# Five weight slots whose residual overwrites the raw weight, in place of four slots and a ring of two raw buffers

## The chip, the cores and the metric

The kernel runs on one core of a Trainium2 chip. The metric is the device time of one execution in microseconds, taken as the median of the runs shown. All arithmetic is float32; matmuls run on float32 operands rounded to the reduced format fp32r.

## What is computed

A batch of one sequence of 256 tokens with 2048 features passes three blocks. The first block has one layer, the second has two, each with an own set of weights. Cut to what matters:

```python
# first block
z = rms_norm(x) @ w_in                      # 2048 x (2048,2048,2048,512,512,2048,2048,2048)
u, g, q, k, v, g_attn, m_lru, m_attn = split(z)
u = depthwise_conv(u); h = rg_lru(u, forward) + rg_lru(u, backward)
y_a = h * silu(g)
y_b = windowed_gqa(rope(q), rope(k), v, sink) * silu(g_attn)
merged = sigmoid(m_lru) * (y_a @ w_proj_a) + sigmoid(m_attn) * (y_b @ w_proj_b)
x = x + rms_norm(merged @ w_out)
# second block, two layers
h = rms_norm_2(x) @ w_in
a = sliding_window_sink_attention(...); b = conformer_conv_module(...)   # 31 taps
c = gated_deltanet(...)                                                  # chunks of 64
x = x + concat(a, b, c gated by silu) @ w_out
```

Nearly all of the arithmetic is the products with the weights. To keep float32 accuracy each product is made of three matmuls: `x_hi*w_hi + x_lo*w_hi + x_hi*w_lo`, where `w_hi` is the weight rounded to fp32r and `w_lo = w - w_hi` is its residual, and the same for x.

## The kernel before

The weights lie in DRAM as 288 slots of 128 x 2048 floats (1 MB): 152 of the first block (`SLOTS_1`), then 68 for each layer of the second (`SLOTS_2`). The class `Ring` streams them. For each slot n there are four steps, each on an engine of its own and each in program order on it:

- `load` (SP): a DMA of slot n from DRAM into one of two raw buffers (`w_raw`, `RAW = 2`). It waits until the residual of slot n-2 is done (semaphore `split`), since that slot was the last to use the same raw buffer.
- `round` (ScalarE, line 273): copies `w_raw` into `w_hi[n % 4]`, rounded. It waits for the transfer (`loaded0`, `loaded1`) and until TensorE has finished slot n-4 (`used`), which had the same `w_hi` and `w_lo`.
- `residual` (VectorE, line 280; in four parts at line 291 in one stage): `w_lo[n % 4] = w_raw - w_hi`. It waits for the rounding.
- `features`, `tokens`, `halves` or `last_tokens` (TensorE, lines 309, 321, 345, 333): 48 matmuls of 256 columns or 24 of 512. They wait for `split` of slot n and increase `used` at the end.

The four steps are placed by hand in each engine's program, `round` and `residual` three slots ahead of the matmuls, between the operations of the stage. The stages of the first block are LRU (slots 0 to 31, in 8 passes of four with gate matmuls at line 1112 after each), keys and values (32 to 39), attention (40 to 71), two gating products and two projections (72 to 135) and the output projection (136 to 151). Those of each later layer, counted from its first slot: C (0 to 7, the input of the 31-tap convolution), KV (8 to 11), Q (12 to 17), ZA (18 to 23), D (24 to 41, the inputs of the delta rule, with the heads' softmax, flips at line 2602, the sum over the convolution at 2623 and the products at 2613 in between), ZB (42 to 45), ZC (46 to 51, with the delta rule's chains of small matmuls and transposes, line 2700 among them) and OUT2 (52 to 67). Between the blocks the first three slots of the next layer are loaded, rounded and split by the block before it.

SP's program holds all transfers in order, also those of constants, gate weights, the stream x that is stored and read back (`x_t`), and waits of its own: for `gates` ahead of each set of gate weights, for `joined` ahead of the store of x between the blocks, for `used` and `added` ahead of the loads and stores of `x_t`. All DMAs go through one queue.

Other names in the rows: L1089 turns the first x; L1112 multiplies by the gate weights and reads `u_all`, which L828 and L832 make (the short convolution); L2501 turns x at the start of the second block; L2540 multiplies the keys `q_raw` by the turning matrix and reads `q_sq`, which L1668 makes; L1755 copies the softmax weights `S` for L2613; L1793 makes `sq` for L2619; L1773 and L2202 make the delta rule's short convolution; L2045 makes the taps of the long one; L1884 scales the keys of the delta rule, and L2234 makes `yb_now`, for which line 2700 waits before its second use.

Of the kernel before, what the change touches and what calls it, by code (L numbers as in the profile page):

```python
# [9 lines left out]
F32 = mybir.dt.float32  # L10
# [14 lines left out]
SLOTS = 4  # L25
RAW = 2
# [220 lines left out]
class Ring:  # L247


    def __init__(self, k, s, first, ready=0, last=None, since=None):  # L250
        self.k, self.s, self.first, self.ready, self.last = k, s, first, ready, last
        self.since = since or record(loaded0=0, loaded1=0, rounded=0, split=0, used=0)
        self.loaded = (s.loaded0, s.loaded1)
        self.odd = 1 if since else 0

    def load(self, sp, n):
        n -= self.ready
        if n < 0 or n + self.ready >= self.last:
            return
        if self.since.split or n >= 2:  # L260
            sp.wait_ge(self.s.split, self.since.split + n - 1)
        raw = (n + self.odd) % RAW
        sp.dma_start(self.k.w_raw[:, raw], self.k.w[self.first + self.ready + n]).then_inc(self.loaded[raw], 16)

    def round(self, act, n):
        if n < self.ready or n >= self.last:
            return
        m = n - self.ready
        raw = (m + self.odd) % RAW
        act.wait_ge(self.loaded[raw], (self.since.loaded1 if raw else self.since.loaded0) + 16 * (m // 2 + 1))  # L270
        if self.since.used or n >= SLOTS:
            act.wait_ge(self.s.used, self.since.used + n - SLOTS + 1)
        act.activation(self.k.w_hi[:, n % SLOTS], self.k.w_raw[:, raw], ACT.Copy).then_inc(self.s.rounded, 1)  # L273

    def residual(self, dve, n):
        if n < self.ready or n >= self.last:
            return
        m = n - self.ready
        dve.wait_ge(self.s.rounded, self.since.rounded + m + 1)
        dve.tensor_tensor(self.k.w_lo[:, n % SLOTS], self.k.w_raw[:, (m + self.odd) % RAW], self.k.w_hi[:, n % SLOTS].bitcast(F32),  # L280
                          ALU.subtract).then_inc(self.s.split, 1)

    def residual_part(self, dve, n, part):
# [3 lines left out]
        m = n - self.ready  # L287
        here = slice(512 * part, 512 * part + 512)
        if part == 0:
            dve.wait_ge(self.s.rounded, self.since.rounded + m + 1)  # L290
        ins = dve.tensor_tensor(self.k.w_lo[:, n % SLOTS, here], self.k.w_raw[:, (m + self.odd) % RAW, here],
                                self.k.w_hi[:, n % SLOTS, here].bitcast(F32), ALU.subtract)
# [3 lines left out]
    def await_slot(self, pe, n):  # L296
        if self.since.split or n >= self.ready:
            pe.wait_ge(self.s.split, self.since.split + n - self.ready + 1)

    def features(self, pe, n, out, x_hi, x_lo, each=None, whole=True):  # L300

        w_hi, w_lo = (w[:, n % SLOTS].rearrange("p (k f) -> p k f", k=KT) for w in (self.k.w_hi, self.k.w_lo))
# [9 lines left out]
    def tokens(self, pe, n, quarter, outs, x_hi, x_lo):  # L312

        w_hi, w_lo = (w[:, n % SLOTS].rearrange("p (k f) -> p k f", k=4) for w in (self.k.w_hi, self.k.w_lo))
# [9 lines left out]
    def last_tokens(self, pe, n, outs, x_hi, x_lo, first_half):  # L324

        w_hi, w_lo = (w[:, n % SLOTS].rearrange("p (k f) -> p k f", k=4) for w in (self.k.w_hi, self.k.w_lo))
# [9 lines left out]
    def halves(self, pe, n, half, outs, x_hi, x_lo):  # L336

        w_hi, w_lo = (w[:, n % SLOTS].rearrange("p (k f) -> p k f", k=8) for w in (self.k.w_hi, self.k.w_lo))
# [28 lines left out]
B1_SEMS = ("loaded0 loaded1 rounded split used "  # L367
# [9 lines left out]
def first_parts(k, t, s):  # L377
# [4 lines left out]
    ring = Ring(k, s, 0, 0, SLOTS_1 + SLOTS - 1)  # L382
# [78 lines left out]
    def sync(sp):  # L461
# [10 lines left out]
        ring.load(sp, 2)  # L472
# [5 lines left out]
        for n in range(3, SLOTS_1 + SLOTS - 1):  # L478
            ring.load(sp, n)
# [809 lines left out]
    "loaded0 loaded1 rounded split used "  # L1289
    "p2_in turn_in soft_in narrow_in cumulate_in levels_in "  # L1290
# [1834 lines left out]
```

## Time and profile before

| | us |
|---|---|
| median of 3 runs | 1966.73 |
| lowest, highest | 1965.78, 1968.35 |
| the profiled execution's own time | 1965.31 |
| its span, first to last instruction | 1963.5 |
| granted TensorE clock, mean | 0.993 |
| TensorE matmul busy | 1917.0 |
| VectorE busy, ScalarE busy | 1263.2, 1105.6 |

The profiled execution took 1.8 us more than its span and 1.4 us less than the median. In the rows that follow, PE is TensorE, DVE is VectorE, ACT is ScalarE, SPq is the queue that issues the DMAs; times are microseconds from the start of the span.

### The profile page before, as it was taken

The numbers are of one execution on the slowest core, as the hardware profiler recorded it, in microseconds if no ns is written. First come the engines' busy times: TensorE is split into PE (matmuls) and PEld (weight loads), VectorE is DVE, ScalarE is ACT, GpSimd is POOL, SyncE is SP. The second block draws the span as 40 slices with busy tenths as digits, with TensorE's granted clock in tenths as the row PEclk, the third lists the DMA queues.
The fourth block names the chain that finished last, engine by engine and source line by source line (L and its number), as shares of the span: only waits on it lengthen the run. The fifth ranks groups of instructions, "written<-read, shape, count | busy, mean of one in ns | idle before, by whom it ended". The sixth has DMA issues, their size and how long they took to land.

```text
span 1963.5 us, 32526 instructions
## 1 busy us (share of the span) xinstructions
PE 1917.0 (98%) x13840; PEld 1726.0 (88%) x13840; DVE 1263.2 (64%) x1771; ACT 1105.6 (56%) x1506; POOL 69.8 (4%) x66
## 2 busy tenths in 40 slices
PE   7999999999999999999899999999999999999998
PEld 6999989999888888888899999898889999888887
DVE  5877856555444444654698988655558888865553
ACT  6777755555543333434656588825464657874451
POOL 0111100000000000000000101100000000010000
PEclk9999999999999999999999999999999999999999
DMA  6444454444455555565544443323555443342153
GB/s 234 181 186 174 160 215 172 154 150 149 177 188 200 193 194 194 184 257 193 204 162 158 161 146 134 120 76 112 213 198 215 164 170 131 131 148 87 66 206 137
DMA packets 52272, 328.61 MB, mean 167 GB/s; under 512 B 7968, under 2 KB 10144, under 8 KB 14368
## 3 DMA queue, kind: packets, MB, share of 16 engines
q1 hardware_dynamic: 52128, 326.54, 46.0%
q8 instruction: 109, 1.79, 0.4%
q14 instruction: 35, 0.29, 0.0%
HBM read 320.23 MB, written 6.29 MB: 166 GB/s over the span
## 4 chain that ended last, share of the span: by engine, by line
PE 83%; DVE 7%; ACT 5%; DMA 3%; issue 2%; SPq 0%; DVEq 0%; ACTq 0%
PE z L321 36%; PE z L309 33%; DMA w_raw<-in_w_dram 3%; DVE w_lo L280 2%; ACT w_hi L273 2%; PE aux L2734 1%; PE aux L1112 1%; DVE conv L2202 1%; PE z L333 1%; DVE acc L2045 1%; PE aux L2739 1%; PE aux L1160 1%; PE aux L2632 1%; PE aux L1177 1%; PE z L345 1%
## 5 line engine op out<-in xcount | busy, mean ns | idle before, releaser
L280 DVE TENSOR_TENSOR w_lo<-w_raw,w_hi 128x2048 fp32r<-128x2048 f32 x274 | 631.2, 2305 | 429.0 <-ACT w_hi L273 428.7
L273 ACT ACTIVATE w_hi<-w_raw 128x2048 fp32r<-128x2048 f32 x286 | 547.7, 1917 | 493.4 <-PE z L321 234.2
L309 PE MATMUL z<-xn_hi,w_hi 128*128 128x256 f32 x2112 | 621.3, 294 | 1.5 <-DVE w_lo L280 0.9
L309 PE MATMUL z<-xn_lo,w_hi 128*128 128x256 f32 x2112 | 598.7, 283 | 0.0
L309 PE MATMUL z<-xn_hi,w_lo 128*128 128x256 f32 x2112 | 598.6, 283 | 0.0
L309 PEld LDWEIGHTS z<-xn_hi,w_hi 128*128 128x128 f32 x2112 | 406.0, 192 | 18.5 <-issue 13.0
L309 PEld LDWEIGHTS z<-xn_lo,w_hi 128*128 128x128 f32 x2112 | 406.4, 192 | 5.0 <-issue 4.3
L309 PEld LDWEIGHTS z<-xn_hi,w_lo 128*128 128x128 f32 x2112 | 405.9, 192 | 0.0
L321 PE MATMUL z<-w_hi,xn_hi 128*128 128x512 f32 x568 | 222.9, 393 | 0.0
L321 PE MATMUL z<-w_hi,xn_lo 128*128 128x512 f32 x568 | 221.1, 389 | 0.0
L321 PE MATMUL z<-w_lo,xn_hi 128*128 128x512 f32 x568 | 221.1, 389 | 0.0
L321 PE MATMUL z<-w_hi,y_hi 128*128 128x512 f32 x368 | 143.6, 390 | 0.0
L321 PE MATMUL z<-w_hi,y_lo 128*128 128x512 f32 x368 | 143.3, 389 | 0.0
L321 PE MATMUL z<-w_lo,y_hi 128*128 128x512 f32 x368 | 143.2, 389 | 0.0
L321 PEld LDWEIGHTS z<-w_hi,xn_lo 128*128 128x128 f32 x568 | 106.6, 188 | 22.3
L321 PEld LDWEIGHTS z<-w_lo,xn_hi 128*128 128x128 f32 x568 | 106.7, 188 | 21.6
L321 PEld LDWEIGHTS z<-w_hi,xn_hi 128*128 128x128 f32 x568 | 106.7, 188 | 21.7
L2045 DVE SCALAR_TENSOR_TENSOR acc<-padded_b,params,acc 128x256 f32<-128x256 f32 x240 | 98.8, 476 | 0.0
L321 PEld LDWEIGHTS z<-w_hi,y_lo 128*128 128x128 f32 x368 | 69.1, 188 | 14.4
L321 PEld LDWEIGHTS z<-w_lo,y_hi 128*128 128x128 f32 x368 | 69.1, 188 | 14.1
L321 PEld LDWEIGHTS z<-w_hi,y_hi 128*128 128x128 f32 x368 | 69.1, 188 | 14.1
L2202 DVE SCALAR_TENSOR_TENSOR conv<-padded,params,conv 128x256 f32<-128x256 f32 x108 | 58.1, 538 | 36.3 <-ACT conv L1773 33.7
(428 smaller groups left out, 2527.1 us busy)
## 6 DMA issues: line engine op xcount, KB each, us to landing
w_raw<-in_w_dram SPq DMA_DIRECT2D x287, 1024.0 KB, 4.8
gate_w<-in_lru_w_dram SPq DMA_DIRECT2D x8, 512.0 KB, 5.8
x_t<-state_dram SPq DMA_DIRECT2D x2, 2048.0 KB, 7.6
x_first<-in_x_dram SPq DMA_DIRECT2D x4, 512.0 KB, 6.4
x_t<-in_x_dram SPq DMA_DIRECT2D x1, 2048.0 KB, 12.1
state_dram<-x_t SPq DMA_DIRECT2D x2, 1024.0 KB, 5.2
pw<-in_pw_dram SPq DMA_DIRECT2D x2, 1024.0 KB, 6.0
state_dram<-x_t SPq DMA_DIRECT2D x8, 256.0 KB, 2.2
```

Of the source, the lines that this page charges most:

```text
L273: act.activation(self.k.w_hi[:, n % SLOTS], self.k.w_raw[:, raw], ACT.Copy).then_inc(self.s.rounded, 1)
L280: dve.tensor_tensor(self.k.w_lo[:, n % SLOTS], self.k.w_raw[:, (m + self.odd) % RAW], self.k.w_hi[:, n % SLOTS].bitcast(F32), ALU.subtract ...
L309: ins = pe.matmul(out, w[:, kk], x[:, kk], start=kk == 0 and j == 0, stop=kk == KT - 1 and j == 2)
L321: ins = pe.matmul(outs[m], x[:, row, t], w[:, kk], start=row == 0 and j == 0, stop=row == KT - 1 and j == 2)
L333: ins = pe.matmul(outs[m], x[:, row, t], w[:, kk], start=False, stop=row == KT - 1 and j == 2)
L345: ins = pe.matmul(outs[m], x[:, row, t], w[:, kk], start=row == 0 and j == 0, stop=row == KT - 1 and j == 2)
L1112: ins = pe.matmul(aux[2 * b + d][:, g * T:g * T + T], gate_w[i % 2][:, b, 2 * d + g], u_all[:, 2 * i + b], start=True, stop=True)
L1160: ins = pe.matmul(aux[2 * p + h][:, b * T:b * T + T], q_turned[:, 2 * p + h, P * b:P * b + P], keys[:, c], start=True, stop=True)
L1177: ins = pe.matmul(aux[2 * p][:, h * T:h * T + T], values[:, kb, P * c:P * c + P], S[p][:, h].rearrange("p b t -> p (b t)")[:, kb * T:kb * ...
L2045: dve.scalar_tensor_tensor(out=acc[:, b], in0=padded_b[:, b, n:n + T], scalar=col(w), in1=acc[:, b], op0=ALU.mult, op1=ALU.add).then_inc(s ...
L2202: dve.scalar_tensor_tensor(out=conv[:, i], in0=padded[:, i, tap:tap + T], scalar=col(w), in1=conv[:, i], op0=ALU.mult, op1=ALU.add).then_i ...
L2632: ins = pe.matmul(aux[m // 2][:, T * (m % 2):T * (m % 2) + T], pw[:, b, P * m:P * m + P], wide[:, b], start=b == 0, stop=b == B - 1)
```

## The change

There are five slots, and the raw ring is gone. `w_lo` is laid on the same memory as `w_raw`: slot n is transferred into place `n % 5`, rounded from there into `w_hi[n % 5]`, and the residual is written over the raw weight. The memory in all is the same (10 buffers of 1 MB). Slots are counted through all layers, so that `place` and `count` are plain functions of the slot's number.

- `load` of slot n waits until TensorE has finished slot n-5 (`used`), and for nothing else.
- `round` waits for the transfer only (one semaphore for each of five places); it no longer waits for `used`.
- `residual` and the matmuls wait as before.
- At the start the loads of slots 2, 3 and 4 are issued at once, behind that of the first gate weights and ahead of five constants; before, the load of slot 2 waited for the residual of slot 0.
- In SP's program the steps tied to a slot are moved by one or two slots: in a layer the load of slot 4 comes ahead of `params`; `turn`, `w12` and `rows` come behind the load of slot 12 and not of 10; the load of `x_t` behind that of slot OUT2+4 (before: +3); the stores of x behind OUT2+11, +13, +17 (before: +10, +12, +16).
- `soft_in`, `cumulate_in` and `levels_in` become one semaphore `tables_in`, and whoever waited for one of them waits for all nine transfers; `turn_in` goes into `narrow_in`, and whoever waited for one waits for all three transfers.

```diff
-SLOTS = 4
-RAW = 2
+SLOTS = 5
+AHEAD = 3
...
     def load(self, sp, n):
-        n -= self.ready
-        if n < 0 or n + self.ready >= self.last:
+
+        if n < self.ready or n >= self.last:
             return
-        if self.since.split or n >= 2:
-            sp.wait_ge(self.s.split, self.since.split + n - 1)
-        raw = (n + self.odd) % RAW
-        sp.dma_start(self.k.w_raw[:, raw], self.k.w[self.first + self.ready + n]).then_inc(self.loaded[raw], 16)
+        if self.count(n) > SLOTS:
+            sp.wait_ge(self.s.used, self.count(n) - SLOTS)
+        sp.dma_start(self.k.w_raw[:, self.place(n)], self.k.w[self.first + n]).then_inc(self.loaded[self.place(n)], 16)
 
     def round(self, act, n):
         if n < self.ready or n >= self.last:
             return
-        m = n - self.ready
-        raw = (m + self.odd) % RAW
-        act.wait_ge(self.loaded[raw], (self.since.loaded1 if raw else self.since.loaded0) + 16 * (m // 2 + 1))
-        if self.since.used or n >= SLOTS:
-            act.wait_ge(self.s.used, self.since.used + n - SLOTS + 1)
-        act.activation(self.k.w_hi[:, n % SLOTS], self.k.w_raw[:, raw], ACT.Copy).then_inc(self.s.rounded, 1)
+        act.wait_ge(self.loaded[self.place(n)], 16 * ((self.first + n) // SLOTS + 1))
+        act.activation(self.k.w_hi[:, self.place(n)], self.k.w_raw[:, self.place(n)], ACT.Copy).then_inc(self.s.rounded, 1)
...
-        dve.tensor_tensor(self.k.w_lo[:, n % SLOTS], self.k.w_raw[:, (m + self.odd) % RAW], self.k.w_hi[:, n % SLOTS].bitcast(F32),
-                          ALU.subtract).then_inc(self.s.split, 1)
+        dve.tensor_tensor(self.k.w_lo[:, at], self.k.w_raw[:, at], self.k.w_hi[:, at].bitcast(F32), ALU.subtract)\
+           .then_inc(self.s.split, 1)
...
         ring.load(sp, 1)
         sp.dma_start(gate_w[0][:].rearrange("p b g n -> p (b g n)"), k.lru_w[0]).then_inc(s.weights0, 16)
-        ring.load(sp, 2)
+        for n in range(2, SLOTS):
+            ring.load(sp, n)
...
-            if n == 10:
+            if n == 12:
                 sp.wait_ge(s.used, since.used + 8)
...
-            if n == SLOT_OUT2 + 3:
+            if n == SLOT_OUT2 + 4:
                 sp.wait_ge(s.used, since.used + SLOT_OUT2)
...
-        k.w_raw = put("w_raw", [P, RAW, SLOT_COLS])
-        k.w_hi, k.w_lo = (put(n, [P, SLOTS, SLOT_COLS], F32R) for n in ("w_hi", "w_lo"))
-        k.y_at = goto(X0 + 4 * SLOT_COLS * (RAW + 2 * SLOTS))
+        k.w_raw, k.w_hi = put("w_raw", [P, SLOTS, SLOT_COLS]), put("w_hi", [P, SLOTS, SLOT_COLS], F32R)
+        k.y_at = goto(X0)
+        k.w_lo = put("w_lo", [P, SLOTS, SLOT_COLS], F32R)
+        goto(k.y_at)
```

## Rows read from the trace of the kernel before

**Rows 1.** The page: busy time, share of the span and instructions of each engine

```profile
PE 1917.0 (98%) x13840; PEld 1726.0 (88%) x13840; DVE 1263.2 (64%) x1771; ACT 1105.6 (56%) x1506; POOL 69.8 (4%) x66
```

**Rows 2.** PE's waits: for whom: us in total, times, longest us

```profile
PE aux L1089 <- DVE x_first L783: 12.8, 1, 12.8
PE aux L2700 <- DVE yb_now L2234: 8.0, 2, 4.0
PE aux L2613 <- ACT S L1755: 4.0, 2, 2.1
...
PE z L2623 <- DVE acc L2045: 2.9, 2, 1.4
PE aux L2540 <- ACT q_sq L1668: 1.4, 2, 0.8
...
PE aux L1112 <- DVE u_all L832: 1.1, 1, 1.1
PE aux L2602 <- DVE S L2183: 1.0, 2, 0.6
PE z L309 <- DVE w_lo L280: 0.9, 1, 0.9
...
PE z L2619 <- ACT sq L1793: 0.6, 1, 0.6
```

**Rows 3.** Waits of the ring: ScalarE's roundings and, last, SP's loads

```profile
ACT w_hi L273 <- PE z L321: 234.2, 74, 3.9
ACT w_hi L273 <- DMA w_raw<-in_w_dram: 200.1, 76, 6.8
...
SPq L263 <- DVE w_lo L280: 1510.1, 259, 14.6
```

**Rows 4.** All instructions of line 263, the loads: from issue to landing

```profile
DMA to landing us min/median/max: 4.6/4.8/10.8
```

**Rows 5.** Critical chain (start, us, what), and from ACT's timeline the last row

```profile
47.60 23.03 PE z L309 x192
...
74.09 23.03 PE z L309 x192
...
511.44 272.02 PE z L321 x1200
...
571.39 1.92 ACT L273 ACTIVATE w_hi<-w_raw 128x2048 fp32r<-128x2048 f32 x1 [3.52 <-PE z L321]
```

**Rows 6.** Timelines of SP and DVE in the first 45 us

```profile
7.10 0.44 SPq L471 DMA_DIRECT2D gate_w<-in_lru_w_dram  x1
21.93 0.33 SPq L263 DMA_DIRECT2D w_raw<-in_w_dram  x1
...
28.69 2.29 DVE L280 TENSOR_TENSOR w_lo<-w_raw,w_hi 128x2048 fp32r<-128x2048 f32 x1 [2.79 <-ACT w_hi L273]
...
42.29 1.53 DVE L832 SCALAR_TENSOR_TENSOR u_all<-padded,params,u_all 128x256 f32<-128x256 f32 x3
```

**Rows 7.** Timeline of ACT in stage KV of the first layer

```profile
1011.23 1.92 ACT L273 ACTIVATE w_hi<-w_raw 128x2048 fp32r<-128x2048 f32 x1 [3.97 <-DMA w_raw<-in_w_dram]
```

**Rows 8.** Timelines of ACT and DVE in stage D, first half

```profile
1129.17 1.92 ACT L273 ACTIVATE w_hi<-w_raw 128x2048 fp32r<-128x2048 f32 x1 [0.83 <-PE z L309]
...
1143.45 1.92 ACT L273 ACTIVATE w_hi<-w_raw 128x2048 fp32r<-128x2048 f32 x1 [1.21 <-DMA w_raw<-in_w_dram]
...
1157.26 1.53 DVE L2202 SCALAR_TENSOR_TENSOR conv<-padded,params,conv 128x256 f32<-128x256 f32 x3 [1.33 <-ACT conv L1773]
```

**Rows 9.** Timeline of ACT in stage D, second half

```profile
1196.93 1.92 ACT L273 ACTIVATE w_hi<-w_raw 128x2048 fp32r<-128x2048 f32 x1 [1.30 <-DMA w_raw<-in_w_dram]
...
1222.64 1.92 ACT L273 ACTIVATE w_hi<-w_raw 128x2048 fp32r<-128x2048 f32 x1 [1.57 <-DMA w_raw<-in_w_dram]
```

**Rows 10.** Timelines of ACT and DVE at the turn from stage ZB to ZC

```profile
1267.45 1.66 ACT L1884 ACTIVATE k_end<-aux,sc 128x128 f32<-128x128 f32 x6 [1.13 <-DVE k_beta L2311]
...
1270.94 2.29 DVE L280 TENSOR_TENSOR w_lo<-w_raw,w_hi 128x2048 fp32r<-128x2048 f32 x1 [3.13 <-ACT w_hi L273]
```

More of the change, by code:

```diff
@@ L277, in residual @@
             return
[L278 to L281 removed]
+        at = self.place(n)
+        dve.wait_ge(self.s.rounded, self.count(n))
+        dve.tensor_tensor(self.k.w_lo[:, at], self.k.w_raw[:, at], self.k.w_hi[:, at].bitcast(F32), ALU.subtract)\
+           .then_inc(self.s.split, 1)
     def residual_part(self, dve, n, part):
@@ L286, in residual_part @@
             return
-        m = n - self.ready
+        at = self.place(n)
         here = slice(512 * part, 512 * part + 512)
         if part == 0:
-            dve.wait_ge(self.s.rounded, self.since.rounded + m + 1)
-        ins = dve.tensor_tensor(self.k.w_lo[:, n % SLOTS, here], self.k.w_raw[:, (m + self.odd) % RAW, here],
-                                self.k.w_hi[:, n % SLOTS, here].bitcast(F32), ALU.subtract)
+            dve.wait_ge(self.s.rounded, self.count(n))
+        ins = dve.tensor_tensor(self.k.w_lo[:, at, here], self.k.w_raw[:, at, here], self.k.w_hi[:, at, here].bitcast(F32), ALU.subtract)
         if part == 3:
@@ L296, in await_slot @@
     def await_slot(self, pe, n):
-        if self.since.split or n >= self.ready:
-            pe.wait_ge(self.s.split, self.since.split + n - self.ready + 1)
+        pe.wait_ge(self.s.split, self.count(n))
     def features(self, pe, n, out, x_hi, x_lo, each=None, whole=True):
-        w_hi, w_lo = (w[:, n % SLOTS].rearrange("p (k f) -> p k f", k=KT) for w in (self.k.w_hi, self.k.w_lo))
+        w_hi, w_lo = (w[:, self.place(n)].rearrange("p (k f) -> p k f", k=KT) for w in (self.k.w_hi, self.k.w_lo))
         if whole:
@@ L312, in tokens @@
     def tokens(self, pe, n, quarter, outs, x_hi, x_lo):
-        w_hi, w_lo = (w[:, n % SLOTS].rearrange("p (k f) -> p k f", k=4) for w in (self.k.w_hi, self.k.w_lo))
+        w_hi, w_lo = (w[:, self.place(n)].rearrange("p (k f) -> p k f", k=4) for w in (self.k.w_hi, self.k.w_lo))
         self.await_slot(pe, n)
@@ L324, in last_tokens @@
     def last_tokens(self, pe, n, outs, x_hi, x_lo, first_half):
-        w_hi, w_lo = (w[:, n % SLOTS].rearrange("p (k f) -> p k f", k=4) for w in (self.k.w_hi, self.k.w_lo))
+        w_hi, w_lo = (w[:, self.place(n)].rearrange("p (k f) -> p k f", k=4) for w in (self.k.w_hi, self.k.w_lo))
         self.await_slot(pe, n)
@@ L336, in halves @@
     def halves(self, pe, n, half, outs, x_hi, x_lo):
-        w_hi, w_lo = (w[:, n % SLOTS].rearrange("p (k f) -> p k f", k=8) for w in (self.k.w_hi, self.k.w_lo))
+        w_hi, w_lo = (w[:, self.place(n)].rearrange("p (k f) -> p k f", k=8) for w in (self.k.w_hi, self.k.w_lo))
         self.await_slot(pe, n)
@@ L477, in sync @@
         sp.dma_start(k.norm_w[:], t["p2"][0, :, P2_NORM:P2_NORM + KT]).then_inc(s.w2_in, 16)
-        for n in range(3, SLOTS_1 + SLOTS - 1):
-            ring.load(sp, n)
+        for n in range(3, SLOTS_1 + AHEAD):
+            if n >= SLOTS:
+                ring.load(sp, n)
             if n % 4 == 3 and n < 28:
@@ L1393, in layer_parts @@
     since = record(**{n: FIRST_COUNTS.get(place[n], 0) + layer * count for n, count in LAYER_COUNTS.items()})
-    ring = Ring(k, s, SLOTS_1 + layer * SLOTS_2, SLOTS - 1, SLOTS_2 + (SLOTS - 1 if more else 0), since)
+    ring = Ring(k, s, SLOTS_1 + layer * SLOTS_2, AHEAD, SLOTS_2 + (AHEAD if more else 0))
     goto = k.goto
@@ L1577, in sync @@
         ring.load(sp, 3)
+        ring.load(sp, 4)
         if layer == 0:
@@ L1580, in sync @@
         sp.dma_start(params[:], k.p2[layer]).then_inc(s.p2_in, 16)
-        ring.load(sp, 4)
         if layer == 0:
```

68 lines of the change are left out of this document (35 added, 33 removed).

## The prediction, made before the result was known

> **What bounds the kernel now.** I read the page's busy times first: the matmuls are busy 1917.0 us of a span of 1963.5 [rows 1]. Whatever the ring does, it can only win back the 46.5 us in which TensorE stands. So the next view is the list of TensorE's own waits [rows 2], and it says two things. TensorE waits for a weight (z L309 <- DVE w_lo L280) once in the whole program, for 0.9 us: the ring as such is never late after the start. All else are waits for products of ScalarE and VectorE: 12.8 us for the first x, 8.0 for `yb_now`, 4.0 for the softmax copies, 2.9 for the taps, and some of about one. The ring can move these only indirectly: its roundings and residuals stand in program order among those operations, and while ScalarE waits inside a rounding, all that is queued behind it waits too.
>
> Third, what the ring waits for [rows 3]: 234.2 us of ScalarE's idle time end when TensorE leaves a slot of line 321, 200.1 when a transfer lands, and SP waits 1510.1 us for residuals before it may issue a load. A late residual makes a late load, and a late load holds up ScalarE. These waits matter only where ScalarE or VectorE is late for TensorE; elsewhere they are spare time.
>
> **The change part by part.** *When a slot can be rounded.* Before: at the release of slot n-4, and not before its transfer has landed, which is issued at the residual of n-2. After: at the landing of a transfer issued at the release of slot n-5. A transfer takes 4.8 us in the median [rows 4]. The shortest slots, 50 of them in 272.02 us, take 5.44 us; those of 256 columns, four in 23.03, take 5.76 [rows 5]. So a rounding may start at release(n-5) + 4.8, before at release(n-5) + 5.44 at best: at least 0.6 us earlier, and more where slots are longer or the transfer used to be late. In the projections this is spare time: a rounding starts when TensorE leaves slot n-4 (after a wait of 3.52 us [rows 5]) and takes 1.92 us, the residual 2.29 [rows 6], and TensorE wants the slot three slots after that release, 16.3 us: 12.1 to spare, gain 0. After, 4.8 + 1.92 + 2.29 = 9.0 of four slots' 21.8 us leave 12.8, so a transfer may take 17.6 us before TensorE feels it; the longest of the run took 10.8 [rows 4].
>
> The price of a transfer has a counterpart in the Trainium skill, page "DMA: Bandwidth & Descriptors", section "Anatomy of one DMA": about 2.0 us fixed, whatever the size, plus the bytes at 436 GB/s, fitted for another kind of queue. That speaks against the change, since the fixed part now lies between TensorE's release and the rounding at every slot. An estimate from that page is 4.4 us for 1 MB; this trace never has less than 4.6 [rows 4], so it agrees within a tenth. With 4.4 every rounding could start another 0.4 us earlier, and the sum below would hardly move.
>
> *The residual in place.* The same instruction with the same shapes, its output on its input's address. No row shows this form on this shape. The nearest is the short convolution at 42.29 [rows 6], which works in place and takes its ordinary 0.5 us each; by it I take 0. As bound I take 0.5 us on either side for each of the two residuals between VectorE's last wait and the taps in stage D (below): 1 us at each of two places, 2 us.
>
> *The start.* The load of slot 2 is issued at 21.93, when the residual of slot 0 is done; its residual runs from 28.69 to 30.98, and TensorE waits 0.9 for it [rows 2, 6]. After, loads 2 to 4 are issued right behind the gate weights of 7.10: even with the longest landing of the run, 10.8, load 2 is there before 20. The 0.9 goes. The short convolution ends at 43.8 behind residuals that waited for ScalarE and so for a transfer, the first of them 2.79 us [rows 6]. It comes earlier by more than the 1.1 us that TensorE waits at L1112. Gain 0.9 + 1.1 = 2.0. The first wait of 12.8 stays: it is x and its norm, and what is new in the queue stands behind x, slots 0 and 1.
>
> *The LRU stage.* SP still waits for `gates` ahead of each set of gate weights, and the next load is queued behind it. The gate matmuls take 74.09 - 47.60 - 23.03 = 3.5 us [rows 5], then half a megabyte goes ahead: the slot is ready 3.5 + 2.4 + 9.0 = 14.9 us after its release and wanted after 3.5 + 23.0. Gain and loss 0.
>
> *Stage KV, both layers.* TensorE waits for `q_sq` twice, 1.4 us in all [rows 2]. That copy stands behind the rounding at 1011.23, which waited 3.97 us for a transfer [rows 7], issued late because the residual before it was: `turn`, `w12`, `rows` and a wait of SP stood ahead of the loads. After, it is issued at a release of TensorE three slots before the copy is wanted, and the 3.97 us cover the 0.8. Gain 1.4. `turn` now stands behind 1 MB more, and TensorE waits for three transfers: issued at the release of slot 7 they need 4.8 and at most 4.8 more, and are wanted three slots later, 17.3. Cover 7.7 us.
>
> *Stage D, first half, both layers.* The taps and the flip (L2623, L2602) cost 2.9 + 1.0 [rows 2]. I followed VectorE back from the taps: it is busy without a break since 1157.26, where it waited for ScalarE's `conv`. ScalarE was held at 1129.17 for TensorE by 0.83 and at 1143.45 for a transfer by 1.21 [rows 8]. Both waits go: the first, since the release of the slot before is 5.76 us or more earlier and the landing 4.8 behind it; the second, since its load hung on a residual. In between the two engines hand over to each other, so the chain moves by 0.83 at least and by all 2.0 at most; I take the second wait's size, 1.25 in each layer: gain 2.5, bounds 1.6 and 3.9.
>
> *Stage D, second half.* ScalarE waits for three transfers, the first by 1.30, the last by 1.57 us, each issued at a residual of VectorE [rows 9]. From the last one it is busy without a break until the softmax copy for which L2613 waits 2.0 us. Bounds for the move are 1.30 and the sum of the three, 4.2; a part of each is taken up by waits for VectorE between them. The middle, 2.75, is more than the 2.0. So the wait goes in both layers, and with it the 0.6 at L2619 on the same chain: gain 4.0 + 0.6 = 4.6, at least 2.6.
>
> *Stage ZB to ZC.* The largest of these waits, 8.0 us at L2700, does not depend on a transfer. TensorE's first pass of that line releases VectorE's scaling, that releases ScalarE's at 1267.45, then in program order a rounding, then VectorE's residual at 1270.94 [rows 10] and some operations more until `yb_now`. The rounding waits for nothing but ScalarE. The ring's work is in the chain, its wait isn't. Stays, 0.
>
> *The join, the output stage, the stores.* The join hangs on the norm at the end of the first block and stays. The load of `x_t` (2 MB) is issued at the same release as before, now behind a load of 1 MB; the next slot's load behind it still has four slots. Stores are tied to `added`, which comes before the next load is due. 0.
>
> *One semaphore for nine tables.* They are issued in stage C; the first who waits is in the next stages, over 12 slots later. 0.
>
> A few waits left out of [rows 2], each under 0.7, may shrink; I take 0.5.
>
> Sum: 2.0 + 1.4 + 2.5 + 4.6 + 0.5 = 11.0 us. Against the profiled execution, 1965.3 - 11.0 = 1954.3; the median stands 1.4 above that one: 1955.7.
>
> **The rivals.** *A: the gain is smaller, because waits only change places.* VectorE is the busier of the two (64% against 56%) [rows 1]. If a wait removed on ScalarE in stage D is found again on VectorE, the start and KV remain: 3.4 us, 1963.3. For it: ScalarE's waits there alternate with waits for VectorE. Against: VectorE waits for ScalarE in that stretch too [rows 8], so the two are one chain.
>
> *B: more, because L2700 moves too.* If the rounding between the two rows of [rows 10] gets its place earlier than I see, up to 8.0 us more: 1948. Against: the row before it is a wait on VectorE.
>
> *C: slower, the landing is now in the path.* From the point where a landing takes longer than a slot, 5.76 us in stage D, roundings start later than before. If transfers there took the mean of median and longest, 7.8 us [rows 4], roundings would be 2.0 us later, and each of the four waits at L2623 and L2613 that much longer: 1966.7 - 3.4 + 4 x 2.0 = 1971.3. Against: paced by TensorE the loads come one by one, and nothing else is queued in stage D.
>
> *D: the change doesn't do what it says.* SP's own waits (gates, joined, added) still stand ahead of some loads, which then aren't paced by TensorE alone. None stands in stage D or at the start; if KV keeps its wait, 1.4 less: 1957.1.
>
> *E: more is won inside the slots.* Slots follow on each other in [rows 5] without a break at the same 5.44 us whatever the other engines do, and no wait of the ring lies in them; so nothing is won there. The Trainium skill, page "Perfetto Trace Analysis", section "Identifying the Most-Contended Engine", says that busy matmul time is a poor measure of what TensorE has left, and to go by the weight loads' busy share. That is 88% here [rows 1], and by the rule more than the 46.5 us could be won, which would end below 1948; 1 in 100.
>
> **How the numbers follow.** The forecast, with its parts off by a few us: 0.72; D, inside it but for 1.4 us: 0.03. A: 0.14. B and E: 0.04. C: 0.07. The likeliest is 1955.7, given as 1956. Its own range is 1953 (upper bounds in D) to 1961 (lower bounds, the price in place, and a scatter of medians of 1.3 us). To hold 8 in 10 it reaches towards A and a little below: 1951 to 1963. A measurement of this kernel can tell from no change about 0.2%, 3.9 us: faster means below 1962.8. Faster 0.79 (forecast, D, B, E), same 0.14 (A), slower 0.07 (C).
>
> **What would show it.** Right: no wait of L309 for w_lo and none at L1112; L2540's, L2613's and L2619's waits gone and L2623's at about 0.6 in each layer; L2700 still at 8.0; ScalarE's waits for TensorE in roundings gone, with waits for transfers of 2 to 3 us in the projections instead; SP waiting for TensorE; loads landing in 4.8 us. Wrong: landings beyond 5.8 us in stage D; residuals longer than 2.3 us; TensorE waiting for w_lo anywhere, above all behind `x_t` in the output stage.

## The result

| kernel | median us | lowest, highest | runs |
|---|---|---|---|
| before | 1967.54 | 1965.78, 1968.44 | 4 |
| after | 1948.28 | 1947.51, 1948.95 | 4 |

The ratio is 0.9903 with a 95% interval of 0.9886 to 0.9920: the change takes 19.3 us away. The forecast was 11.0 us, and 1948.3 lies below the range of 1951 to 1963. The profiled execution of after took 1948.24 us with a span of 1946.5, beside 1965.31 and 1963.5 of before: 17.0 us between the spans.

The page of after, its busy times (compare [rows 1]), the chain that ended last, the costliest groups and the issues of loads:

```profile
span 1946.5 us, 32242 instructions
PE 1911.4 (98%) x13840; PEld 1723.3 (89%) x13840; DVE 1262.8 (65%) x1771; ACT 1102.3 (57%) x1506; POOL 69.9 (4%) x66
...
PE 90%; DVE 5%; ACT 3%; issue 1%; DMA 1%; SPq 0%; DVEq 0%; ACTq 0%
...
L280 DVE TENSOR_TENSOR w_lo<-w_raw,w_hi 128x2048 fp32r<-128x2048 f32 x274 | 631.9, 2308 | 387.4 <-ACT w_hi L272 387.1
L272 ACT ACTIVATE w_hi<-w_raw 128x2048 fp32r<-128x2048 f32 x286 | 546.6, 1916 | 391.5 <-DMA w_raw<-in_w_dram 391.4
...
w_raw<-in_w_dram SPq DMA_DIRECT2D x287, 1024.0 KB, 4.8
```

TensorE stands 1946.5 - 1911.4 = 35.1 us where it stood 46.5: 11.4 us less idle time, beside the 11.0 of the forecast. But its busy time fell as well, by 5.6 us with the same 13840 matmuls. That is where the forecast was short.

TensorE's waits in after (us in total, times, longest; compare [rows 2]):

```profile
PE aux L1089 <- DVE x_first L783: 12.8, 1, 12.8
PE aux L2700 <- DVE yb_now L2234: 8.0, 2, 4.0
PE aux L2501 <- DVE x_t L1990: 3.6, 1, 3.6
PE z L2623 <- DVE acc L2045: 1.4, 2, 1.1
PE z L2806 <- DVE vnew L2382: 1.3, 2, 0.7
PE aux L2501 <- DVE raw_lo L1996: 1.2, 2, 1.0
PE aux L2789 <- DVE w_t L2377: 0.6, 2, 0.3
```

The waits at L309 for `w_lo`, at L1112, L2540, L2613, L2602 and L2619 are gone, and of the 2.9 us at L2623 1.4 are left. L2700 stands at 8.0, as forecast. The ring's waits (compare [rows 3]; line 263, the load, is now 266):

```profile
SPq L266 <- PE z L307: 988.9, 142, 18.9
SPq L266 <- PE z L319: 670.5, 127, 8.6
```

For its loads SP now waits for TensorE alone, ScalarE's roundings wait for transfers (391.4 us), and the transfers still land in 4.8 us.

To see where the time went without the noise of the whole, I read from the traces when TensorE left each slot (the events of `used`), and took the length of each stretch. Where nothing waits such a stretch repeats within 0.03 us from execution to execution, so small differences can be trusted there. Where something waits, one execution is one sample. A stretch is named by stage and layer; D a is the first twelve slots of stage D (24 to 35), D b the last six with the first slot of ZB. b2 is a second profile of the kernel before, e1 and e2 are experiments below.

```
us                     before     b2    e1    e2  after
slots 1 to 4            29.20  30.07  29.32 26.77  26.75
rest of first block    881.42 881.42 880.95 881.44 880.65
KV, layer 0             26.77  26.75  25.77 24.75  24.75
D a, layer 0            86.62  86.66  87.39 86.62  85.67
D b, layer 0            53.52  51.95  51.98 49.93  49.94
first ZC slot, layer 0  19.21  19.70  19.54 18.39  19.22
C, layer 1              47.37  48.77  47.37 47.37  47.37
KV, layer 1             26.28  26.10  25.14 24.75  24.75
D a, layer 1            86.76  86.62  85.42 86.66  84.84
D b, layer 1            54.36  54.42  54.23 50.11  49.94
first ZC slot, layer 1  18.27  19.47  19.57 18.45  18.43
```

Slot 0 (24.2 to 25.3 us) and stage C of layer 0 (59.6 to 60.1) vary without relation to the kernel; all stretches not listed agree within 0.03. D a varies too: in the eight profiles below that share the code of after around it (after, e4, e6, e6f, e7, e8, e9 and e12) it takes 84.98 to 85.91 us in layer 0 and 84.69 to 86.33 in layer 1. Before to after: start 2.5 (less 0.4 in slot 0), first block 0.8, KV 2.0 + 1.5, D a 1.0 + 1.9, D b 3.6 + 4.4.

### The profile page after: what moved, and what is told of

Its sections match the earlier page's. It is cut to its first block, busy times and chain, and to the rows that moved or that the text cites. A ratio compares the mean times of both kernels' runs of the same rounds, so it can differ in the third digit from the quotient of the medians.

```text
span 1946.5 us, 32242 instructions
## 1 busy us (share of the span) xinstructions
PE 1911.4 (98%) x13840; PEld 1723.3 (89%) x13840; DVE 1262.8 (65%) x1771; ACT 1102.3 (57%) x1506; POOL 69.9 (4%) x66
## 4 chain that ended last, share of the span: by engine, by line
PE 90%; DVE 5%; ACT 3%; issue 1%; DMA 1%; SPq 0%; DVEq 0%; ACTq 0%
PE z L307 38%; PE z L319 37%; PE aux L2734 1%; PE aux L1112 1%; PE z L343 1%; DVE w_lo L280 1%; DVE acc L2045 1%; PE z L331 1%; ACT w_hi L272 1%; DVE conv L2202 1%; PE aux L2739 1%; PE aux L1160 1%; PE aux L2632 1%; PE aux L1177 1%; PE z L2561 1%
## 5 line engine op out<-in xcount | busy, mean ns | idle before, releaser
L280 DVE TENSOR_TENSOR w_lo<-w_raw,w_hi 128x2048 fp32r<-128x2048 f32 x274 | 631.9, 2308 | 387.4 <-ACT w_hi L272 387.1
L272 ACT ACTIVATE w_hi<-w_raw 128x2048 fp32r<-128x2048 f32 x286 | 546.6, 1916 | 391.5 <-DMA w_raw<-in_w_dram 391.4
```

Of the source, the lines that this page charges most:

```text
L272: act.activation(self.k.w_hi[:, self.place(n)], self.k.w_raw[:, self.place(n)], ACT.Copy).then_inc(self.s.rounded, 1)
L280: dve.tensor_tensor(self.k.w_lo[:, at], self.k.w_raw[:, at], self.k.w_hi[:, at].bitcast(F32), ALU.subtract)\
```

## The experiments

Runs are compared with the kernel before and with after; dummy instructions are marked as such, their results are used by nothing.

**e1: tie the loads to the residual again.** In `load`, behind the wait for `used`:

```
+        if self.count(n) > 2:
+            sp.wait_ge(self.s.split, self.count(n) - 2)
```

> The changed kernel, but the transfer of slot n also waits until VectorE has made the residual of slot n-2 (in the kernel before it waited for just that). Theory (the gain of 19 us comes from transfers that no longer hang on VectorE's residual two slots back, and from the granted clock that is kept where a wait goes): nearly all of the gain is lost, 1960 to 1968 us, the TensorE waits at the two features of the D stage (4.0 and 2.9 us before) and in the KV stage are back, and with them the stretches of 3.41 us at a granted clock of 0.5 behind 1234 and 1743 us. Rival (the gain comes from ScalarE's rounding, which no longer waits for TensorE to leave the slot): this stays at 1948 to 1951 us.

Measured: 1961.83 us (1960.26 to 1965.26, ten runs; before beside it 1966.88), ratio 0.9975, interval 0.9966 to 0.9984. The wait gives back 13.5 of the 19.3 us. Its waits:

```profile
PE aux L2702 <- DVE yb_now L2236: 8.1, 2, 4.0
PE aux L2615 <- ACT S L1757: 4.0, 2, 2.1
PE aux L2503 <- DVE x_t L1992: 3.6, 1, 3.6
PE z L2625 <- DVE acc L2047: 2.3, 2, 1.4
```

L2615 is L2613 of the other kernels, L2625 is L2623. The softmax wait is back in full, and in the table D b, part of KV and the start are back too. Two things expected are not: behind the softmax wait of layer 0 the clock does not drop (D b takes 51.98 us there), and the waits at L2540 in stage KV stay away; what is back in KV are waits for `xn_lo` of 0.3 us and less. The theory holds for the main part. Of the 5 us that e1 keeps, e2 explains some.

**e2: let ScalarE wait for TensorE again.** In `round`, behind the wait for the transfer:

```
+        if self.count(n) > 4:
+            act.wait_ge(self.s.used, self.count(n) - 4)
```

> The changed kernel, but ScalarE's rounding of slot n waits also until TensorE has left slot n-4, as in the kernel before. Theory (the gain is in the transfers that are free of VectorE): a loss of 0 to 3 us, 1948 to 1951 us, since ScalarE comes to most roundings when slot n-4 has long been left. Rival (the gain is in ScalarE not waiting for TensorE): 1960 to 1968 us.

Measured: 1951.04 us (1950.15 to 1951.50), 2.8 us above after. The table says where, by stretch: the first block is at 881.44 as before, D a at 86.62 and 86.66 as before, and all else is as after, but for the first ZC slot, whose length goes with that of a clock drop in it. So the change is at least two changes. The loads' freedom from VectorE is worth the start, D b and the rest of KV; ScalarE's freedom from TensorE removes two short waits in the first block and gives D a. In D a of layer 0 both are needed: e1, which has only ScalarE's freedom, takes 87.39 us there against 85.67. Its 85.42 in layer 1 lies within the scatter of that stretch. The waits at L2540 are absent in e1 and in e2 alike. So neither freedom is needed for them; the fifth slot, or the loads that no longer stand behind `turn`, `w12` and `rows`, would do, and no run here separates these.

**e7: undo the start alone.** Loads 2, 3 and 4 wait for `split` 1, 2 and 3, as before.

```
+        sp.wait_ge(s.split, 1)
+        ring.load(sp, 2)
...
+            if n < SLOTS:
+                sp.wait_ge(s.split, n - 1)
+            ring.load(sp, n)
```

Loads 3 and 4 stand behind the five constants again, as before.

> The changed kernel, but the transfers of slots 2, 3 and 4 wait at the start for the residual of slots 0, 1 and 2, as they did in the kernel before. It prices the start alone. Theory: the waits of TensorE for the residual of slot 2 (0.9 us) and for the copies of the first gate (1.1 us) are back, 1.6 to 2.6 us more than the changed kernel, 1950 to 1951 us. Rival (the start's gain is of another kind, as the order of the transfers): within 0.7 us of the changed kernel.

Measured: 1952.28 us (1950.43 to 1952.87), 4.0 above after, twice the forecast. Its waits in the first 80 us:

```profile
PE aux L1090 <- DVE x_first L784: 12.9, 1, 12.9
PE aux L1113 <- DVE u_all L833: 1.5, 1, 1.5
PE z L307 <- DVE w_lo L280: 1.5, 2, 0.9
```

Here `w_lo` is late twice. The stretch of slots 1 to 4 took 30.47 us in e7, and 29.20, 30.07, 29.32 and 31.82 in before, b2, e1 and e3; wherever the loads are free it took 26.75 to 26.77. The start was worth 3.4 us in the mean of these five (3.0 without e3, in which a clock drop of 3.41 us follows the wait at L1112), and the profile from which I forecast it was its cheapest.

**b2: the kernel before, once more.**

> The kernel before, unchanged, profiled once more. Its runs beside e1 to e4 spread over 6.6 us (1963.3 to 1969.9) where those of the changed kernel spread over 1.4. Theory (the price of a wait: idle time, and the granted clock of 0.5 for 3.41 us behind the 2 us waits in the D stage): the waits are where they stood in the first profile, within 0.3 us each, and so are the two drops of the clock behind 1234 and 1743 us; where the time of the whole differs, the difference sits at the start or at the border of the two layers. Rival (waits and drops fall by chance): other waits, the drops elsewhere or gone.

Measured: 1967.48 us, span 1965.7. The waits are where they were, but not all within 0.3 us (L1112 1.5 instead of 1.1, a new one of 1.2 at the border of the layers, seen in C above), and the clock is not the same. Two windows of b2 around the waits at L2613 (busy us of PE, PEld, DVE, ACT, POOL, granted clock, DMA share, GB/s):

```profile
1229.00:1239.00 10.00, 8.05 (x64) 7.07 (x62) 7.72 (x10) 9.91 (x16) 0.00 (x0) 1.00 0.30 107
1738.00:1748.00 10.00, 7.93 (x55) 7.31 (x55) 7.92 (x10) 9.91 (x16) 0.00 (x0) 0.83 0.34 116
```

and the same windows of the first profile of before:

```profile
1229.00:1239.00 10.00, 8.02 (x55) 7.15 (x54) 8.13 (x12) 9.91 (x16) 0.00 (x0) 0.83 0.34 113
1738.00:1748.00 10.00, 7.93 (x55) 7.42 (x54) 6.96 (x9) 9.91 (x16) 0.00 (x0) 0.83 0.46 157
```

TensorE stands 2 us in each of the four. In three of them 3.4 us of work behind the wait ran at a granted clock of 0.5 (1.2 GHz): 55 matmuls fall into the window, and 64 into the one at full clock. In the table D b of layer 0 is 53.52 us with the drop and 51.95 without: the drop costs 1.57 us. So a 2 us wait often, not always, brings a slower clock after it. Theory and rival are each half right.

**e3: fill the wait in the kernel before.** 15 dummy matmuls in the wait at L2613 of both layers:

```
+            if n == 41:
+                pe.wait_ge(yout[0], yout_since[0] + 3)
+                fill(aux[0], 15)
             if n >= 26 and n % 3 == 2:
                 mix((n - 26) // 3)
```

> The kernel before, with 15 matmuls added (128x128 by 128x256, their result is used by nothing) just ahead of the last product with the values in the D stage of both layers, where TensorE then waits 4.0 us for ScalarE's copy. They fill the wait: TensorE is busy in it, and nothing else moves. Theory (a wait of 4 us there costs its idle time and then about 1.7 us more, since the granted clock was 0.5 for 3.41 us right behind it, at 1234.8 and 1743.4 us): the drops behind the two waits are gone, and the time is 2.5 to 4 us below the kernel before although the wait is still paid in full. Rival (the clock drops are not caused by these waits, or cost nothing): within 1 us of the kernel before, the drops still there.

Measured: 1967.97 us (1965.47 to 1972.41, ten runs) beside 1966.88, ratio 1.0007, interval 0.9997 to 1.0017: by the time of the whole nothing is won. The window around the first wait has no drop,

```profile
1234.00:1240.00 6.00, 6.00 (x51) 5.49 (x51) 4.21 (x5) 5.97 (x11) 0.00 (x0) 1.00 0.49 172
```

and D b takes 51.80 and 52.18 us, 1.7 and 2.2 less than in before; in the second layer the wait of 0.6 us at L2619 is absent as well, so that the 2.2 are not the clock's alone. The profiled execution, the longest of the ten, lost more than that where nothing was edited: 2.6 us in slots 1 to 4 and 5.3 at the border of the layers, with a clock drop of 3.41 us behind a wait at each place. The kernel before scatters by more (1963.3 to 1973.4 in 33 runs) than the effect looked for, so I repeated the test on the kernel after, whose runs lie within 1.5 us.

**e6 and e6f: make the wait again, then fill it.** e6 puts 31 dummy copies of one column on ScalarE ahead of its last softmax copy (`warm` is widened to 32 columns for them); e6f adds the 15 matmuls of e3.

```
             if h == 5:
+                for j in range(31):
+                    act.activation(k.warm[:, j + 1:j + 2], k.eps[:], ACT.Copy)
             copy_weights(h)
```

> The changed kernel, with 31 one-column copies without use put on ScalarE right ahead of its last copy of the attention weights in the D stage of both layers, some 3.1 us at 0.10 us each by the row of 128x4, so that TensorE waits there about 2.0 us, as in the kernel before. Theory (such a wait costs its idle time, 0.15 us beside it, and 1.7 us for a granted clock of 0.5 in the 3.41 us behind it): 3.5 to 4.2 us for each layer, 1955 to 1957 us, with drops of the clock at about 1229 and 1730 us. Rival (a wait costs its idle time alone): 2.0 to 2.2 us for each layer, 1952 to 1953 us.

> As e6, with 15 matmuls added (128x128 by 128x256, their result is used by nothing) in the wait of TensorE that e6 makes. ScalarE's delay is the same, TensorE is busy in it. Theory (1.7 us of each wait's price is the clock behind it): 3 to 4 us faster than e6, 1952 to 1953 us, no drop there. Rival (the clock costs nothing): as e6 within 0.7 us.

Measured: e6 1957.38 us (1954.77 to 1958.36), e6f 1955.28 (1953.98 to 1956.50), a difference of 2.1 that by these runs alone is not certain. The windows of e6, then of e6f:

```profile
1229.00:1239.00 10.00, 8.26 (x58) 7.80 (x57) 5.15 (x9) 9.91 (x24) 0.00 (x0) 0.83 0.30 107
1730.00:1740.00 10.00, 7.91 (x55) 7.40 (x54) 5.66 (x11) 9.91 (x36) 0.00 (x0) 0.83 0.30 107
```

```profile
1229.00:1239.00 10.00, 10.00 (x82) 9.45 (x82) 5.33 (x9) 9.91 (x28) 0.00 (x0) 1.00 0.29 107
1730.00:1740.00 10.00, 9.72 (x81) 9.16 (x80) 5.69 (x10) 9.91 (x32) 0.00 (x0) 1.00 0.28 107
```

By stretch: D b takes 49.94 in after, 53.24 and 53.60 in e6 (waits of 1.74 and 2.09 us in it), 51.75 and 52.09 in e6f. So ScalarE's lateness costs 1.81 and 2.15 us, and the clock behind it 1.49 and 1.51. Together that is 3.30 and 3.66 us for each layer, where the theory had 3.5 to 4.2 and the rival 2.0 to 2.2: the theory holds, a little below its range in one layer. The 1.5 us are the price of the drop, and b2 (1.57) and e3 (1.7 in layer 0) agree. Of the 3.0 us that e6f saves there 0.7 were paid back in layer 0: the first ZC slot, which holds the 4 us wait at L2700, took 18.36 us in e6 and 19.05 in e6f, with a clock drop of 3.41 us there in e6 and of 6.83 in e6f. That the one drop was longer because the other was filled away is not shown: at the same place it is 6.83 us in after and e7 and 3.41 in e2 and e12, and in layer 1 e6f gains 0.4 in that slot. Both kernels also took 2.75 us more in the first block than after, where nothing was added; e12 is about that.

**e4: fill the waits at L2700 in after.** 32 dummy matmuls ahead of the keys by token.

```
                 if r:
+                    fill(z[3], 32)
                 keys_by_token(r)
```

> The changed kernel, with 32 such matmuls without use added where TensorE waits 4.0 us ahead of the keys by token of the second half (the wait that rival B was about; a drop of the granted clock to 0.5 for 6.83 us and 3.41 us stands near it at 1266.4 and 1768.2 us). Theory (the drops come from the waits): they are gone and the time falls by 3 to 5 us, to 1943 to 1945 us. Rival (the drops have another cause, as the small matmuls in the stage behind): 1948 us within 1, the drops still there.

Measured: 1946.60 us (1945.55 to 1946.75), 1.7 less than after; ratio to before 0.9895. Both windows are at full clock now (after, then e4):

```profile
1260.00:1275.00 15.00, 10.98 (x140) 9.99 (x138) 9.88 (x18) 6.63 (x13) 1.41 (x2) 0.77 0.20 71
1760.00:1775.00 15.00, 10.99 (x145) 9.93 (x144) 10.82 (x20) 6.17 (x13) 1.41 (x2) 0.89 0.18 71
```

```profile
1260.00:1275.00 15.00, 14.43 (x197) 13.18 (x197) 11.21 (x21) 5.97 (x13) 1.44 (x2) 1.00 0.21 72
1760.00:1775.00 15.00, 14.43 (x202) 13.25 (x200) 11.78 (x22) 5.39 (x13) 1.44 (x2) 1.00 0.22 72
```

The drops came from the waits, as the theory says, but the gain is 1.6 and 0.8 us by stretch, half of what I expected. The drop of 6.83 us begins 1.7 us before the wait ends, and a part of it passes while TensorE stands anyway; and a new wait of 0.36 us for `v_beta` stands behind in each layer. Dummy work pays 1.7 us here.

**e10: four slots instead of five.** `SLOTS = 4`, all else as after.

> The changed kernel with four slots of weights in place of five, the residual still in place. A slot's transfer then starts when TensorE leaves the slot four back: of the 17 us that three slots take it keeps 4.8 us for the transfer, 1.9 for the rounding and 2.3 for the residual, and 8 us are left for the queues of ScalarE and VectorE, where the changed kernel has 14. Theory (what counts is that the transfer doesn't hang on VectorE's residual; depth is a margin): some of the small waits of the D stage come back, 1950 to 1958 us, and far below the kernel before. Rival (the gain is the fifth slot): 1962 us or more.

Measured: 2054.65 us (2049.99 to 2056.48), ratio 1.0437, interval 1.0421 to 1.0452: 87 us slower than the kernel before. Both theory and rival fall short. The longest of ScalarE's waits, in e10 and then in after:

```profile
ACT w_hi L272 <- DMA w_raw<-in_w_dram: 726.0, 226, 10.5
```

```profile
ACT w_hi L272 <- DMA w_raw<-in_w_dram: 391.4, 139, 8.3
```

The trace shows rival C of the prediction, one slot further. ScalarE's program rounds slot n+3 early in slot n. With five slots that transfer may start when slot n-2 is left, with four when slot n-1 is left, which is the moment slot n begins; it lands 4.8 us later, and until then ScalarE stands, in 226 of 286 roundings and for 3.2 us in the mean, with the softmax copies, the emptied banks and the roots of the norms queued behind it. TensorE never waits for `w_lo` in e10; it waits 9.6 us for `S` at L2602, 19.6 at L2700, 7.1 for `xn_lo`, and stands 111 us in all. My margin (8 us) was reckoned up to the moment TensorE wants the slot. The one that decides is up to ScalarE's place for the rounding: by this estimate it is in after about one slot, 5.4 to 7 us, less 4.8; in e10 it is nothing.

**e8: another order from ZB to ZC.** The largest wait that the ring doesn't reach, 8.0 us at L2700, hangs on VectorE's last gate product. ScalarE's rounding goes ahead of the ends of the keys, its opening of the last ZB slot ahead of the next rounding, and VectorE's gate products ahead of what TensorE does not yet need:

```
         open_b(1)
+        ring.round(act, SLOT_ZB + 6)
         end_keys(0)
-        ring.round(act, SLOT_ZB + 6)
         open_b(2)
...
+        branch_gate(1)
         scale_keys(0)
         ring.residual(dve, SLOT_ZB + 6)
-        branch_gate(1)
         branch_gate(2)
...
+                if kk == 0 and n == SLOT_ZC:
+                    branch_gate(3)
```

> The changed kernel with another order at the border of the ZB and ZC slots of both layers: ScalarE rounds the weights of slot ZC+2 ahead of the ends of the keys and opens the last ZB slot ahead of the next rounding; VectorE makes its last gate product ahead of the products of the first chain. The wait of 4.0 us for that gate product, which TensorE has in both layers, should go, and with it the clock drops of 6.83 and 3.41 us there, worth 1.7 us together by e4. Theory: 7 to 10 us less than the changed kernel, 1938 to 1941 us. Rival A (a wait takes the place of that one: the transfer of slot ZC+2 lands too late, or the keys' ends): 1944 to 1949 us. Rival B (the 4 us of TensorE were cover for work that is late behind it, the first products of the chains): 1942 to 1946 us, with new waits between 1265 and 1300 us.

Measured: 1939.84 us (1939.36 to 1940.42), ratio to before 0.9854, interval 0.9837 to 0.9870; 8.4 us less than after. Its waits there:

```profile
PE aux L2712 <- ACT k_end L1884: 2.3, 2, 1.1
PE aux L2725 <- DVE v_beta L2318: 0.7, 2, 0.4
```

The 8.0 us are gone, 3.0 us of new waits stand behind them, the clock stays at full there, and the first ZC slot takes 14.5 us in place of 19.2 and 18.4. The theory is right, with a little of both rivals: 2.3 us for the ends of the keys (A) and 0.7 for `v_beta` (B).

**e9: e8 and 29 dummy matmuls in the wait of 3.64 us where the second block begins.**

```
+            for _ in range(29):
+                pe.matmul(aux[0][:, 0:T], k.xn_hi[:, 0, 0:P], k.xn_hi[:, 0], start=True, stop=True)
             for j in range(4):
                 turn_x(j)
```

> e8 with 29 matmuls (128x128 by 128x256, their result is used by nothing) in TensorE's wait of 3.64 us for the joined inputs at the start of the layers, 3.5 us of work. A drop of the clock to 0.5 for 6.83 us begins 1 us before that wait ends and runs over work behind it. Theory (the drop is the wait's): it goes, 1.5 to 2.5 us less than e8, 1937.3 to 1938.3 us. Rival (as between e6 and e6f, where a drop that was filled away came back in part behind the next wait): 1939 to 1940 us, a drop behind the wait of 1.25 us.

Measured: 1939.04 us (1938.82 to 1939.93), 0.8 less than e8, by these runs not to be told from it. The clock drop is gone (window 930 to 945 of e8, then of e9), but it had lain over short waits, and stage C of layer 0, which holds it, takes 59.59 us in place of 60.05: the drop had cost 0.5. The theory's 1.5 to 2.5 us are missed; the time is the rival's, without the rival's drop.

```profile
930.00:945.00 15.00, 9.87 (x55) 8.76 (x54) 9.97 (x21) 10.19 (x25) 1.05 (x1) 0.77 0.27 97
```

```profile
930.00:945.00 15.00, 12.21 (x87) 10.62 (x85) 10.66 (x22) 9.94 (x26) 1.06 (x1) 1.00 0.32 113
```

**e12: 124 bytes.** The kernel after with `warm` 32 columns wide and no added instruction.

```
-        k.post_root, k.warm = put("post_root", [P, 2]), put("warm", [P, 1])
+        k.post_root, k.warm = put("post_root", [P, 2]), put("warm", [P, 32])
```

> The changed kernel with 31 unused columns added to one small tile, so that the tiles of the first part placed behind it (yb_hi and yb_lo among them, whose 128x128 blocks TensorE loads in the PB stage) lie 124 bytes further. No instruction is added or moved. In e6 and e6f the products of the PB stage began every 234 ns where they begin every 227 ns in the changed kernel, 2.9 us over its 16 slots, and nothing else was changed there. Theory (the place of the loaded operand makes it): the same 234 ns and 2.5 to 3.5 us more than the changed kernel, 1951 to 1952 us. Rival (it came from the copies added on ScalarE, or by chance): 227 ns and 1948 to 1949 us.

Measured: 1950.45 us (1949.53 to 1951.28), 2.2 above after. The groups of the PB stage, 770 to 830 us, in e12 and then in after (busy us, mean ns):

```profile
L319 PE MATMUL z<-w_hi,yb_lo 128*128 128x512 f32 x83 | 32.9, 396 | 0.0
L319 PE MATMUL z<-w_lo,yb_hi 128*128 128x512 f32 x83 | 32.9, 396 | 0.0
```

```profile
L319 PE MATMUL z<-w_lo,yb_hi 128*128 128x512 f32 x85 | 33.1, 389 | 0.0
L319 PE MATMUL z<-w_hi,yb_lo 128*128 128x512 f32 x84 | 32.7, 390 | 0.0
```

From start to start they take 234 ns in e12 and 227 in after. The first block is 2.76 us longer. The theory holds: `yb_hi` and `yb_lo` are the only operands of these matmuls that lie elsewhere, and the products of the same form with `xn` or `y`, which were not moved, keep their 227 ns.

## Why the prediction was wrong

*The start* (forecast 2.0). The mechanism was right, e7 shows it; the term was mis-sized. Load 2 is there at 19.0 as I reckoned, but loads 2, 3 and 4, issued half a microsecond apart, landed after 11.7, 13.6 and 15.6 us, longer than the 10.8 that I took for the longest; it cost nothing. The profile had 2.5 us of it, the mean of five executions with tied loads 3.4, e7's median 4.0. I took one execution's waits as the size of something that hangs on how 1 MB transfers fall in the first 50 us.

*The LRU and the rest of the first block* (forecast 0). Right but for 0.8 us in stage PB, two waits of TensorE for `merged` (L1256) of 0.2 us that e2 brings back.

*Stage KV* (1.4). The waits at L2540 are gone as forecast. Of my two reasons for the late load, VectorE's residual and what stood ahead of it in SP's program, the first is not enough: the waits stay away in e1, whose loads hang on that residual again. The stretches became 2.0 + 1.5 = 3.5 us shorter. Part of the rest is three waits for `xn_lo` of 0.2 us each. These and the two for `merged` are 1.1 us that I had put at 0.5 as "a few waits left out". And the list shows of every wait less than it costs. In b2:

```profile
1013.89 0.28 PE L345 MATMUL z<-w_hi,xn_lo 128*128 128x256 f32 x1
1014.79 1.10 PE L2540 MATMUL aux<-q_raw,turn 128*128 128x512 f32 x2 [0.61 <-ACT q_sq L1668]
```

The matmul at 1013.89 is drawn 0.28 us long, but the next of its kind begins 0.12 us after it. TensorE could have begun at 1014.01 and begins at 1014.79: 0.78 us late, of which the idle column has 0.61. So each wait costs 0.16 us more than it shows, and one under 0.16 us shows nothing. Before has 31 waits over 0.02 us behind the first one, after has 16: 15 x 0.16 = 2.4 us that my sum had at zero. This is an estimate from the rows; no run tests it by itself.

*Stage D, first half* (2.5, measured 2.9). Right in size, in part by luck. The waits at L2602 are gone, and of L2623 1.4 us are left where I had 1.2, but as 1.1 and 0.3 and not as 0.6 twice, and among the eight profiles with this code they add up to between 0.7 and 1.9. The reading of ScalarE's waits was not exact (1.21 us went into the sum as 1.25, and one of 0.43 at 1134.93 was left out). The two that I named, for TensorE and for the transfer, both matter: e2, which brings back the first, loses 2.8 of the 2.9, and e1, which brings back the second, 1.7 in layer 0. They don't add up; one alone is enough to be late.

*Stage D, second half* (4.6, measured 8.0). The step that failed. The waits went exactly as forecast, L2613's 4.0 and L2619's 0.6. Not in the sum was what came behind them: in before 3.41 us at a granted clock of 0.5 followed each wait at L2613, 1.5 us each by e6 and e6f, 3.0 in all. The hidden 0.16 us of three waits make most of the rest. The page's line of the clock shows nine tenths or more in all 40 slices; the drop is seen only in a window of a few us set behind the wait. [rows 1] gave busy time as fixed, and I concluded that the ring "can only win back the 46.5 us in which TensorE stands". That sentence is wrong: busy time at half clock can be won back too.

So, between the two profiled executions: 11.4 us of idle time, 3.0 of clock, 2.4 of hidden halves of waits, together 16.8 of 17.1. The other 2.2 of the 19.3 us lie between before's first profile (1965.3) and its median (1967.5): probably the start, and the border of the layers, where b2 lost 1.4 and e3 5.3 us, and none of the profiles of the changed kernel with five slots lost anything. In b2 and e3 the chain of work that ends TensorE's wait there runs through a load that SP issued behind the stores of x, which waited for VectorE; it landed after 6.3 us, and a rounding, a residual and the last sum into `x_t` followed. Which part of the change takes that away is not shown; e1, with tied loads, didn't have these waits in its profile.

*The transfer behind TensorE's release* (cost 0). Right: 4.8 us, no wait for `w_lo`. Two loads of stage D landed after 5.9 and 6.0 us, beyond the 5.8 that I had named as a sign of being wrong, and cost nothing. But the 12.8 us I gave it to spare were reckoned to the wrong place, as e10 shows; the change stands nearer to the edge than I said.

*The residual in place* (0, bounds of 1 us): right, 2308 ns in the mean and 2305 before. *L2700, the join, the output stage* (0): right.

*The rivals.* A (waits change places): no. C (the landing in the path): not at five slots, and 106 us over after at four. E: the rule of the Trainium skill, page "Perfetto Trace Analysis", section "Identifying the Most-Contended Engine", would have had gains inside the slots, and the time ended at the edge of where E put it. This section of the Trainium skill asks for the share of the peak arithmetic beside that of the weight loads; no profile here prints it. E was right that busy time is not fixed, for 5.6 of the 17.0 us came out of it. Yet by this trace that is not headroom inside the slots: the weight loads' share rose from 88 to 89%, the slots between the waits take the same time to 0.03 us, and by the account above 5.4 of the 5.6 us lie next to waits, in the clock behind them and in the drawn tail before them. B's time came out as well, without its mechanism: L2700 stayed. A time that agrees with a rival proves nothing for it.

## What to carry to other kernels

Price a wait of TensorE at its idle time, plus the hidden tail of the matmul before it (0.16 us here), plus what the granted clock does behind it; look at a window of a few us behind each wait of about 2 us or more, since a mean clock of 0.993 hides it. When a buffer's release is moved to another engine, reckon the margin up to the place of the first instruction that waits for the refill in its engine's queue, not up to the last consumer: one slot fewer made this kernel 5% slower than with five. And once a ring is free of the other engines, the waits that are left belong to the order of the operations, and a few lines moved (e8) brought 8.4 us more.

## What I had not expected of the hardware

The granted clock falls to 0.5 behind some waits of 2 us and not behind others of the same length: behind three of four in before and b2, one of two in e1, both in e6 (waits of 1.74 and 2.09 us). Matmuls without use in the wait keep it at full (e3, e6f, e4). The length of a drop varies as well, 3.41 or 6.83 us behind the same 4 us wait at L2700.

In stage PB a 128x512 matmul whose loaded 128x128 block was moved by 124 bytes in its partition begins every 234 ns instead of every 227, 3%, and 2.2 us of the whole (e12). The products of stage C, which stream the equally shifted `raw_hi` and `raw_lo` past loaded weights, kept their 120 ns. Which offsets are the good ones was not tried.
